# Scan of the hybrid layers: first score in an earlier step, decay broadcast over 128 rows, sums of squares one step later

## What is computed

```python
def ssd_scan(xdt, la, bm, cm):                 # 4 groups of 8 heads of 64, chunks of 128 tokens
    def step(state, inp):
        xc, lac, bc, cc = inp
        acs = jnp.cumsum(lac, axis=1)
        seg = acs[:, :, None] - acs[:, None, :]
        lmat = jnp.where(mask, jnp.exp(jnp.where(mask, seg, 0.0)), 0.0)
        cb = jnp.einsum('bign,bjgn->bijg', cc, bc)
        y = jnp.einsum('bijgr,bjgrp->bigrp', cb[..., None] * lmat, xc)
        ...
ys = ys + d_skip * xs
ys = ys * silu(z)
ysg = ys.reshape(bsz, s, 4, 512)
ysg = ysg * rsqrt(mean(ysg * ysg, axis=-1, keepdims=True) + EPS)
```

## Time and profile before

| | us |
|---|---|
| median of 3 runs | 2571.84 |
| the profiled execution | 2575.09 |
| its span | 2573.3 |
| TensorE busy in the span | 2243.2 (87%) |
| VectorE busy | 1232.2 (48%) |
| ScalarE busy | 926.1 (36%) |

### The profile page before, as it was taken

One profiled execution on the slowest core, in us unless ns is written; L12 is line 12 of the kernel. 1 busy time (PEld: TensorE's weight loads), 2 busy tenths in 40 slices (PEclk: granted clock), 3 DMA queues, 4 the chain that ended last, 5 costly groups with the idle time before them and its releaser, 6 DMA issues.

```text
span 2573.3 us, 38038 instructions
## 1 busy us (share of the span) xinstructions
PE 2243.2 (87%) x16792; PEld 1685.1 (65%) x16792; DVE 1232.2 (48%) x1761; ACT 926.1 (36%) x1324; POOL 1.4 (0%) x6
## 2 busy tenths in 40 slices
PE   8998666666989666666999999999999999999998
PEld 7773222112745211112799998999979999999996
DVE  4543212121873111111566589666466647876654
ACT  4141000001232000000455477654445546865543
POOL 0000000000000000000000000000000000000000
PEclk9999888888989878888999999999999999999999
DMA  6419999999358999999734434445544435344542
GB/s 287 165 60 391 428 427 428 428 427 427 124 237 346 428 428 427 428 428 428 290 143 179 178 136 144 171 181 184 188 174 171 164 140 193 134 160 166 192 173 103
DMA packets 48204, 662.95 MB, mean 258 GB/s; under 512 B 5344, under 2 KB 5600, under 8 KB 7968
## 3 DMA queue, kind: packets, MB, share of 16 engines
q1 hardware_dynamic: 47808, 659.17, 63.9%
q0 software_dynamic: 224, 1.26, 0.1%
HBM read 659.36 MB, written 1.05 MB: 257 GB/s over the span
## 4 chain that ended last, share of the span: by engine, by line
PE 59%; DMA 27%; DVE 7%; ACT 6%; issue 1%; DVEq 0%; ACTq 0%
DMA ring<-w_dram 27%; PE ps L2494 8%; PE ps L2496 8%; PE ps L2495 8%; PE ps L1949 3%; PE ps L908 3%; PE ps L1372 2%; PE ps L2912 2%; PE ps L2913 2%; PE ps L2914 2%; PE ps L940 2%; ACT r L2470 1%; PE ps L3562 1%; PE ps L3563 1%; PE ps L3564 1%
## 5 line engine op out<-in xcount | busy, mean ns | idle before, releaser
L2481 DVE TENSOR_TENSOR r<-ring,r 128x1024 fp32r<-128x1024 f32 (+2 forms) x376 | 503.8, 1350 | 326.4 <-ACT r L2470 325.7
L2470 ACT ACTIVATE r<-ring 128x1024 fp32r<-128x1024 f32 (+2 forms) x376 | 427.4, 1154 | 261.8 <-PE ps L2496 107.4
L908 PE MATMUL ps<-ring 128*32 128x512 f32 x1936 | 295.7, 742 | 190.3 <-DMA ring<-w_dram 190.0
L2494 PE MATMUL ps<-r 128*128 128x256 f32 x1504 | 433.9, 289 | 1.8 <-DVE r L2705 1.7
L2495 PE MATMUL ps<-r 128*128 128x256 f32 x1504 | 425.3, 283 | 0.0
L2496 PE MATMUL ps<-r 128*128 128x256 f32 x1504 | 425.2, 283 | 0.0
L908 PEld LDWEIGHTS ps<-ring 128*32 128x32 f32 x1936 | 60.5, 122 | 411.9 <-DMA ring<-w_dram 210.2
L2494 PEld LDWEIGHTS ps<-r 128*128 128x128 f32 x1504 | 287.9, 191 | 7.7 <-issue 2.9
L2495 PEld LDWEIGHTS ps<-r 128*128 128x128 f32 x1504 | 288.1, 192 | 0.4
L2496 PEld LDWEIGHTS ps<-r 128*128 128x128 f32 x1504 | 288.0, 192 | 0.0
L1154 DVE TENSOR_TENSOR arena<-ps,arena 128x512 f32<-128x512 f32 x16 | 11.1, 692 | 446.2 <-PE ps L908 446.2
(11 more groups left out here) (497 smaller groups left out, 3675.2 us busy)
## 6 DMA issues: line engine op xcount, KB each, us to landing
ring<-w_dram SPq DMA_DIRECT2D x301, 2048.0 KB, 23.3
arena<-w_dram SPq DMA_DIRECT2D x6, 2048.0 KB, 14.5
ring<-w_dram SPq DMA_DIRECT2D x4, 1024.0 KB, 4.9
arena<-w_dram SPq DMA_DIRECT2D x2, 1536.0 KB, 7.3
x<-x_dram SPq DMA_DIRECT2D x2, 512.0 KB, 3.7
ring<-w_dram SPq DMA_DIRECT2D x2, 512.0 KB, 10.7
out_dram<-x SPq DMA_DIRECT2D x4, 256.0 KB, 2.0
cst<-w_dram SPq DMA_DIRECT2D x1, 973.0 KB, 22.7
```

What stands on the lines that cost most here:

```text
L908: r = pe.matmul(p[32 * j:32 * j + 32, :], xg[:, k, j * CAP:(j + 1) * CAP], w[kk * 4 + j], start=k == 0, stop=k == 7)
L2470: a.activation(hi, w, ACT.Copy).then_inc(*S.up(f"hi {s}"))
L2481: v.tensor_tensor(lo, w, hi.bitcast(F32), SUB).then_inc(*S.up(f"lo {s}", *(["free " + name] if last else [])))
L2494: pe.matmul(out, hi[:, k, :], HH[:, k, :], start=k == 0, stop=False)
```

## The change

Three edits, all in the scan of both hybrid layers.

The `cum` matmuls now use all 128 rows of `CSR` and `EACH`. Rows 64 to 127 of both are set to zero once per layer by one VectorE subtraction of a constant from itself (`REST`, 64 partitions x 288). The product is the same.

The first score of a group is issued by VectorE right behind the triangle products in step 2, no longer in step 3 behind the input line's cut. The other three stay.

In groups 0 to 2, everything from the sum of squares over partitions onward is put one step later (`apart`): TensorE's L2826 from step 14 to 15, ScalarE's logarithm and exponential from 15 to 16 and its rounding copy from 17 to 18, VectorE's four scalings from 16 to 17 and its subtraction from 17 to 18. Squares and VectorE's own additions stay in step 12. The scan then has 19 steps for these groups, within the input's 20.

```diff
@@ hyb_bufs
-    s.CSR, s.EACH = K.CSR[0:64, 0:256], K.CSR[0:64, 256:288]
+    s.CSR, s.EACH, s.REST = K.CSR[:, 0:256], K.CSR[:, 256:288], K.CSR[64:128, :]
@@ hyb_pe, cum
-                r = pe.matmul(p[:, i * 256:(i + 1) * 256], s_.EACH[:, hh:hh + 1].broadcast_to([64, 128]), s_.CSR,
+                r = pe.matmul(p[:, i * 256:(i + 1) * 256], s_.EACH[:, hh:hh + 1].broadcast_to([128, 128]), s_.CSR,
                               start=True, stop=True)
@@ hyb_pe, ssd_do
         yield
         yield
+        yield from apart(g)
         yield from sums(s_.SQ, f"s{g}", inner(g))
@@ hyb_act
-        a.activation(s_.CSR, s_.CST, ACT.Copy).then_inc(*S.up(st + " cs upper"))
+        a.activation(s_.CSR[0:64, :], s_.CST, ACT.Copy).then_inc(*S.up(st + " cs upper"))
...
-        yield from rstd(s_, f"s{g}", f"{st} yz{g}", 3)
+        yield from rstd(s_, f"s{g}", f"{st} yz{g}", 4 if g < 3 else 3)
@@ hyb_dve, steps
-        v.tensor_tensor(s_.EACH, K.par("ident", 0, 128)[0:64, 0:32], K.par("ident", 0, 128)[0:64, 32:64], ADD).then_inc(
+        v.tensor_tensor(s_.REST, K.par("ident", 0, 288)[64:128, :], K.par("ident", 0, 288)[64:128, :], SUB).then_inc(*S.up())
+        v.tensor_tensor(s_.EACH[0:64, :], K.par("ident", 0, 128)[0:64, 0:32], K.par("ident", 0, 128)[0:64, 32:64], ADD).then_inc(
             *S.up())
@@ hyb_dve, ssd_do
-        yield
-        for hp in range(4):
+
+        def score(hp):
             se = s_.SE[hp % 2]
             v.wait_ge(*K.after(f"{st} decay{g}{hp}"))
             if hp == 0:
                 own()
             v.tensor_tensor(se, se, s_.CB.unsqueeze(1).broadcast_to([128, 2, 384]), MUL).then_inc(
                 *S.up(f"{st} se{g}{hp}"))
+
+        score(0)
+        yield
+        for hp in range(4):
+            if hp:
+                score(hp)
             yield
             yield
             v.wait_ge(*K.after(f"{st} y{g}{hp}"))
...
         yield
+        yield from apart(g)
         v.wait_ge(*K.after(f"{st} rss{g}"))
```

## The result

The changed kernel takes 2580.86 us (median of 7 runs, 2577.74 to 2582.3) against 2571.84: 1.0028 of the time before, interval 1.0019 to 1.0038, which is 4.9 to 9.8 us more. The forecast was 2574.1 and the range ended at 2578.5. The direction of the forecast's sum held, its size didn't.

The account below looks back on a forecast made before the run. It took TensorE to set the time, with little room on VectorE and ScalarE. Per layer, group 0 -0.65, two passages +2.24, group 3 -0.43 gave +1.16; two layers +2.3 on 2571.84: 2574.1 us, range 2564.5 to 2578.5.

Parts of the forecast that it names:

- Part 1: `cum` matmuls over 128 rows: TensorE alone saves 4.2 us a layer, 0.38 per lone pair, 0.19 behind y products.
- Rival D: At the `cum` matmuls, zero rows save no time in the array: +2.5 us a layer, 2576.8 us, chance 0.08.
- Part 2: First score one step earlier: it comes 1.1 us earlier, the second score does not, so y1 can gain only 0.17.
- the margin of y1: In groups 1 and 2, y1 could start at 1551.49 behind the second score and starts at 1551.66: 0.17 us.
- ScalarE's 0.67: ScalarE's idle time at 1548.70 in group 1, taken to absorb part of the later y1 start of 1.92 us.
- Part 3: Sums one step later in groups 0 to 2: sum product loses its wait, scalings 2.09 us later, y1 +1.92.
- the tile's wait: Third tile of the gate product in group 3 waits 0.71 us for a split that ends later.
- Per passage: From one group to the next: +1.92 at y1, -0.19 for a pair, -0.61 for the sum, together +1.12 us.
- -0.19 and -0.61: TensorE's savings per passage: 0.19 us from a `cum` pair after y1, 0.61 from the sum product's vanished wait.
- Group 0, forecast at -0.65: Group 0 of each layer: -0.19 us for one pair after the second score, -0.46 for the sum product's wait.
- Rival C: The 2.09 us delay passes on undiminished at the fourth score: +3.1 us a layer, 2578.0 us, chance 0.15.
- The signs that the forecast named: Among them: `cum` steps of 0.12 us, scalings 2.1 later, ScalarE idle 2.9, y0 and y1 waits over 1.

Follow-up runs that it names:

- the pair of kernels with 3.4 + 1.4 and 4.8 us of waits: The changed kernel without its third edit, 2568.08 us, and that kernel with only TensorE's sum product one step later, 2569.4 us.
- part 3 alone: The kernel before with only the third edit, sums and scalings one step later in groups 0 to 2: 2592.0 us, 1.0073.
- the 64 rows: The changed kernel with the `cum` broadcast back on 64 rows, the other two edits kept: 2584.56 us, 1.0042.

## Why the prediction was wrong

**Part 1, right in size, wrong in place.** The steps around a lone pair are now 0.11, 0.23 for both of the pair and 0.12, as worked out. The Trainium skill, "TensorEngine Tiling (Array Packing)", "Key Properties", says that a change of tiling mode drains the engine, and the trace agrees: with the change of rows gone, the steps of 0.21 and 0.22 are 0.11 and 0.12. The extension gives 1.12 us a layer in group 3 (forecast 1.14), and 0.00 in the passages, where the forecast kept 0.19. Rival D, that zero rows save nothing in the array, is out. The added subtraction cost nothing that shows.

**Part 2, too small.** The forecast gave it 0.17 at most, from the margin of y1. Alone it gives 0.31, through the third `cum` pair and ScalarE. The forecast took ScalarE's 0.67 before that pair for slack; it was a link of the loop.

**Part 3, the delay right, the credits wrong.** The delay of 2.09 us (the scalings start 2.12 after the exponential instead of 0.03, and the passage is 39.86 against 37.76), the idle 2.9 (2.87) and the sum without a wait came out. The tail of group 3 is 82.14 against 82.58, -0.44 where -0.43 was forecast, and that is luck: the tile's wait in it is 1.16 rather than 0.71, and the 0.50 that TensorE gains at group 2's sum, booked in the forecast under the passage, falls here and makes up for it. The y waits grew to over 1 us at y0, as forecast (2.46 and 2.45). y1 of group 2 waits 1.1; y1 of group 1 doesn't, since TensorE at the low clock gets there late. The step that failed is the sum "Per passage": it started from y1 of one group and let TensorE's -0.19 and -0.61 behind y1 carry over to the next, which gave +1.12; in the passages the runs show nothing for either. The walk ended at TensorE and wasn't followed round the loop of ScalarE and VectorE. TensorE then waits for the next first score by what it had saved, as the pair of kernels with 3.4 + 1.4 and 4.8 us of waits shows. Without a fall of the clock a passage is 39.86: +1.77, which is the delay of 2.1 less the 0.33 of part 2, instead of +1.12. Group 0, forecast at -0.65, lies in the same loop: from its first tanh to the next it takes 37.84, before 37.86.

**Not in the forecast at all: the clock.** The forecast had y0 wait for over 1 us and priced that as waiting time only; it gave no size, and the 2.5 us that came brought the low clock with them in three of four places.

The difference from forecast, over two layers: passages 4 x (1.77 - 1.12) = 2.6; group 0 2 x 0.63 = 1.3; clock 0.48 + 0.52 + 0.49 = 1.5. Together 5.4, and 2.3 + 5.4 = 7.7, against 7.6 measured in the scans. Rival C had the right sign and the nearly right mechanism (the delay passed on undiminished), but it placed it at the fourth score and kept group 0's gain; and it stood at 0.15. The signs that the forecast named came, but for the wait at y1 of three groups, and passages longer than 38 us fit +1.77 as well as +1.12: they could not tell the forecast from C. The forecast read TensorE as what sets the time because it is busy 36.98 of 38 us, and noted that the other two have little room, but did not ask whether they close a loop; a loop through two engines that are each partly idle (ScalarE busy 30.31, VectorE 33.72), crossing TensorE for 1.35 us only, was the bound.

## What to carry to other kernels

Where an engine waits a little in every round (0.6 us here), a saving on it counts only if it isn't the one that waits: follow the chain backward from one mark to the same mark one round earlier, and count only what lies on that loop. Then take the two cheapest tests of the loop: remove a wait on the busiest engine and see whether another wait grows by the same amount (1.4 us here), and remove a wait inside the loop and see whether the round gets shorter (0.90 us for 0.79). And an order that leaves TensorE standing for two microseconds or more may cost more than the standstill.

## What the runs showed of the hardware

After standing for 2.45 or 2.46 us before y0, TensorE was granted 0.50 of its clock (1.2 GHz) for 3.4 us, in three of the four places of after; the fall came between the start of y0 and 1.1 us behind it. In the fourth, with a standstill of 2.45 us, it stayed at 1.00. With part 3 alone the low level lasted 6.8 us at a standstill of 3.19 us (it began before the standstill ended) and 3.4 us behind one of 3.36 us; with the 64 rows it lasted 6.8 us at one of 2.06 us and didn't come behind 2.22 us. These two kernels did the same in both layers. Where TensorE stood 1.31 us or less, no scan of any kernel here shows a fall, and filling the time with matmuls prevented it. A fall cost its passage 0.5 us in after (40.33 against 39.86), 2.2 us with the 64 rows (42.00 against 39.83), and 1.4 to 2.9 us with part 3 alone (41.63 to 43.05 against the estimate of 40.18). What decides whether it comes, and for how long, stays open: the length of the standstill alone doesn't.
